# Two groups of on-chip buffers moved to other start addresses: activations by 96 bytes, shared buffers by 160 bytes in each partition

## The chip, the cores and the metric

The kernel runs on one core of one Trainium2 chip. Its time is device microseconds (us) of one launch, the median of three runs. The on-chip memory SBUF has 128 partitions; a buffer lies at the same byte address in each of them, and the kernel writes these addresses by hand.

## The reference

The program is a small language model's forward pass over 256 tokens of width 1024, in float32, three layers in a row.

- Layer 1: RMS norm; one projection to 2840 columns; compressed, selected and windowed attention (8 heads) beside differential attention (4 heads); output projection; squared-ReLU MLP of width 4096.
- Layer 2: the same frame with 16-head block attention and a second MLP of width 4096.
- Layer 3: one projection to 7696 columns that feeds a gated linear recurrence (1280 channels, a convolution of 4 taps, a scan) and 16-head forgetting attention; two branch projections, a merge and an output projection; then a gated feed-forward part of width 3072 with a convolution of 3 taps; a last norm.

```python
for i in range(DEPTH):                                   # layers 1 and 2
    hn = rms_norm(x, norm_mix[i])
    mix = even_mixer(hn, ...) if i % 2 == 0 else odd_mixer(hn, ...)
    x = x + mix
    x = x + sqrelu_mlp(rms_norm(x, norm_mlp[i]), mlp_w1[i], mlp_w2[i])
x = rms_norm(x, norm_final)
# layer 3
proj = rms_norm_2(x, mix_norm_pre) @ w_in
y_a = gelu(ga) * rg_lru(causal_dwconv(xa, ...), ...)
y_b = forgetting_attention(q, k, v, f_logit + b_forget)
merged = sigmoid(g_a + b0) * (y_a @ w_proj_a) + sigmoid(g_b + b1) * (y_b @ w_proj_b)
x = x + rms_norm_2(merged @ w_out, mix_norm_post)
up = causal_dwconv(rms_norm_2(x, ffn_norm_pre) @ w_up, ...)
x = x + rms_norm_2((gelu(gate) * val) @ w_down, ffn_norm_post)
```

Nearly all of the work is the product of activations with weight matrices.

## The kernel before

**Weights.** Every weight matrix is cut into slabs of 1024 rows by 256 columns (1 MiB). SP's queue loads each slab into one of five slots of `raw` (`slab`, L471), ScalarE writes a rounded copy to `w_hi` (`split_hi`, L698), and VectorE writes the remainder `w_lo = raw - w_hi` over the raw slab (`split_lo`, L1026). Both halves have the type float32r.

**Activations.** They are split in the same way into a high and a low part, float32r too, in one of a few buffers: `act_hi`/`act_lo` (the inputs of nearly all first products), `hid_hi`/`hid_lo` (the MLP's hidden layer), `mix_hi`/`mix_lo` (attention output), `ya_hi`/`ya_lo`, `m2_hi`/`m2_lo` (named `m_hi`/`m_lo` in the rows) and `h2_hi`/`h2_lo` (named `h_hi`/`h_lo`).

**The product.** TensorE runs `gemm` (L1532), one slab a call. For each of the slab's eight chunks of 128 rows and for both halves of its columns it issues three matmuls, high by high, high by low and low by high, each preceded by its own load of a 128x128 block into the array:

```python
passes = ((w_hi, x_hi), (w_hi, x_lo), (w_lo, x_hi))
...
ins = pe.matmul(dst, lhs, rhs, ...)      # L1561; lhs is loaded, rhs streams past it
```

Normally `lhs` is a block of the weights and `rhs` is a 128x256 piece of the activations (1024 bytes in each partition). Where `tok_major` is set, the roles are exchanged: `lhs` is a block of the activations and `rhs` is a 128x256 piece of the weights. This is so for the values of the attention stages, the gates, and the whole last stage (`f_dn`). In the rows a name such as `ps_gemm<-act_hi,w_hi` is the normal form and `ps_gemm<-w_hi,act_hi` the exchanged one (the streaming operand stands first). A full slab is 48 matmuls. All of these products have the line L1561 in the profile.

**Order.** The order of the work is written out by hand for each engine; semaphores join the engines. In the three attention stages a table (`FILL`) puts pieces of the products between the scores, transposes and value products of each pair of heads, so that TensorE works while VectorE and ScalarE do the softmax. Outside of them (the MLPs, the projections of layer 3, its feed-forward part) the products follow one another with no other work on TensorE.

**Placement.** `place` (L176 and what follows) puts each buffer at `top[0]`, the next free byte rounded up to 32. First come the weights' slots, the bias, `x`, small tables, then `act_hi` and `act_lo`. Behind them lie 8 KiB of scratch (`tmp0`: `sq`, `sq_sum`, `up_r`, `up_q`, `prob`, `sig_a`, `f_logsig`), and from `arena` on about 70 KiB that the stages share in turn (`hid`, `mix`, `ya`, `m2`, `h2`, queries, keys, values, `xa_pad` and all others made by `ar`). The starts that the code gives:

| buffers | start before | remainder by 64 | by 128 |
|---|---|---|---|
| `w_lo`, `w_hi` | 16512, 57472 | 0 | 0 |
| `eps_ones` (a table of constants) | 130272 | 32 | 96 |
| `act_hi`, `act_lo` | 132800, 140992 | 0 | 64 |
| `tmp0` and all in it | 149184 | 0 | 64 |
| `arena`; `hid_hi`, `mix_hi`, `h2_hi`, `xa_pad` start there | 157376 | 0 | 64 |

All pieces that a matmul of L1561 reads lie a multiple of 512 bytes behind its buffer's start, so that a buffer's remainders are those of all its pieces.

Of the kernel before, what the change touches and what calls it, by code (L numbers as in the profile page):

```python
# [141 lines left out]
def build(nc, ctx, t, out):  # L142
# [5 lines left out]
    top = [base]  # L148

    def place(name, shape, dt=F32, at=None):  # L150
        size = int(np.prod(shape[1:])) * 4
        if at is None:
            at = top[0]
            top[0] = -(-(at + size) // 32) * 32
        return nc.alloc_sbuf_tensor_at(name, shape, dt, offset=at)
# [23 lines left out]
    rs_o = place("ffn_rs", [P, TB])  # L179
    fcq = place("f_cum_q", [P, TB, 16])  # L180
    fw = place("conv_f", [P, 4, 2 * NH2])
    act_hi = place("act_hi", [P, NX, T], F32R)
    act_lo = place("act_lo", [P, NX, T], F32R)
    tmp0 = top[0]
    arena = tmp0 + 8 * K
    assert arena + 70 * K <= 229344, arena + 70 * K

# [1740 lines left out]
```

## Time and profile before

| | |
|---|---|
| median of three runs | 1252.53 us (1247.95 to 1256.39) |
| the profiled execution's own time | 1244.96 us |
| its span, first to last instruction | 1243.2 us |
| mean granted TensorE clock | 0.962 of full speed |
| TensorE matmul / weight load busy | 1158.9 us (93%) / 1116.4 us (90%) |
| VectorE, ScalarE, GpSimd busy | 796.4, 586.6, 147.4 us |
| read from HBM | 192.86 MB, 156 GB/s over the span |

A matmul counts as busy from its start to its modelled end (about 0.28 us), and the next one starts before that end. What a matmul costs in a long row of them is therefore the distance between two starts, which is had from the number of matmuls in a stretch, not from the busy time.

### The profile page before, as it was taken

How to read it: one execution, taken by the hardware profiler on the slowest of the kernel's cores; microseconds unless marked ns; L12 is line 12 of the kernel's file. 1: busy time of each engine (PE TensorE's matmuls, PEld its weight loads, DVE VectorE, ACT ScalarE, POOL GpSimd, SP SyncE). 2: the span in 40 equal slices, each digit the busy share in tenths (PEclk: the TensorE clock that was granted, in tenths of full speed). 3: DMA queues.
4: the chain of work that ended last, by engine and by line, in shares of the span. 5: the costliest groups of instructions: out<-in, count | busy, mean ns of one | idle time of the engine just before them, and what ended most of it. 6: DMA issues, size and time to landing. Idle time of an engine off the chain costs nothing.

```text
span 1243.2 us, 21636 instructions
## 1 busy us (share of the span) xinstructions
PE 1158.9 (93%) x9407; PEld 1116.4 (90%) x9407; DVE 796.4 (64%) x1131; ACT 586.6 (47%) x823; POOL 147.4 (12%) x83
## 2 busy tenths in 40 slices
PE   6799888999999999999999999999977979999997
PEld 5798668999999899999999999999975879999997
DVE  6436546877454665787654788776554677888852
ACT  4146654443334464444433556654344446666531
POOL 3000004000031000400022202400060021110100
PEclk8879889999999999999999999999988998999999
DMA  8934205555555443656555371654951353656550
GB/s 218 221 101 136 69 2 162 177 187 187 188 186 169 136 137 106 200 179 194 181 192 178 121 206 41 197 158 150 318 189 35 103 169 105 201 173 218 177 195 36
DMA packets 198771, 195.71 MB, mean 157 GB/s; under 512 B 9692, under 2 KB 196757, under 8 KB 198677
## 3 DMA queue, kind: packets, MB, share of 16 engines
q1 hardware_dynamic: 194116, 190.72, 49.2%
q10 hardware_dynamic: 4560, 3.62, 1.0%
q8 instruction: 74, 1.21, 0.4%
q14 instruction: 21, 0.16, 0.0%
HBM read 192.86 MB, written 1.46 MB: 156 GB/s over the span
## 4 chain that ended last, share of the span: by engine, by line
PE 77%; DVE 9%; SPq 5%; DMA 3%; POOL 2%; ACT 1%; issue 1%; DVEq 0%; ACTq 0%; POOLq 0%
PE ps_gemm L1561 67%; PE ps_score L1626 2%; PE ps_out L1653 2%; DVE w_lo L1026 2%; PE ps_trans L1638 2%; PE ps_score L1837 2%; DMA f_bias<-cum_scr 2%; DVE prob L1066 1%; SPq L509 1%; PE ps_gemm L1731 1%; POOL f_bias L657 1%; SPq L553 1%; DVE act_lo L1032 1%; DMA raw<-in_w_in 1%; DVE prob L1095 1%
## 5 line engine op out<-in xcount | busy, mean ns | idle before, releaser
L1561 PE MATMUL ps_gemm<-act_hi,w_hi 128*128 128x256 f32 x1640 | 467.3, 285 | 27.0 <-DVE act_lo L1032 21.2
L1561 PE MATMUL ps_gemm<-act_lo,w_hi 128*128 128x256 f32 x1640 | 461.8, 282 | 0.0
L1561 PE MATMUL ps_gemm<-act_hi,w_lo 128*128 128x256 f32 x1640 | 461.5, 281 | 0.0
L1026 DVE TENSOR_TENSOR w_lo<-raw,w_hi 128x2048 fp32r<-128x2048 f32 (+2 forms) x179 | 409.5, 2295 | 69.1 <-ACT w_hi L698 68.7
L698 ACT ACTIVATE w_hi<-raw 128x2048 fp32r<-128x2048 f32 (+2 forms) x179 | 332.7, 1862 | 204.0 <-DMA raw<-in_mlp_w 97.9
L1561 PEld LDWEIGHTS ps_gemm<-act_hi,w_hi 128*128 128x128 f32 x1640 | 311.6, 190 | 35.8 <-issue 30.4
L1561 PEld LDWEIGHTS ps_gemm<-act_lo,w_hi 128*128 128x128 f32 x1640 | 311.6, 190 | 0.3
L1561 PEld LDWEIGHTS ps_gemm<-act_hi,w_lo 128*128 128x128 f32 x1640 | 311.3, 190 | 0.2
L1561 PE MATMUL ps_gemm<-hid_hi,w_hi 128*128 128x256 f32 x512 | 143.1, 280 | 0.0
L1561 PE MATMUL ps_gemm<-hid_hi,w_lo 128*128 128x256 f32 x512 | 143.1, 279 | 0.0
L1561 PE MATMUL ps_gemm<-hid_lo,w_hi 128*128 128x256 f32 x512 | 142.8, 279 | 0.0
L1561 PEld LDWEIGHTS ps_gemm<-hid_hi,w_lo 128*128 128x128 f32 x512 | 96.2, 188 | 0.0
L1561 PEld LDWEIGHTS ps_gemm<-hid_lo,w_hi 128*128 128x128 f32 x512 | 96.0, 188 | 0.0
L1561 PEld LDWEIGHTS ps_gemm<-hid_hi,w_hi 128*128 128x128 f32 x512 | 95.9, 187 | 0.0
L755 ACT ACTIVATE prob<-prob,nmin 128x256 f32<-128x256 f32 (+3 forms) x128 | 54.3, 425 | 41.4 <-DVE nmin L1066 41.2
L623 POOL TENSOR_TENSOR sq_sum<-x 128x512 f32<-128x512 f32 x5 | 12.8, 2570 | 488.9 <-DVE x L1230 251.9
L831 ACT ACTIVATE hid_hi<-up_r 128x512 fp32r<-128x512 f32 x32 | 20.2, 632 | 93.3 <-DVE up_r L1248 93.3
L1066 DVE CUSTOM_DVE_ANT_0 prob<-ps_score,bias 128x128 f32<-128x128 f32 (+1 forms) x96 | 25.7, 323 | 48.6 <-PE ps_score L1626 48.6
L1561 PE MATMUL ps_gemm<-w_hi,act_hi 128*128 128x256 f32 (+1 forms) x192 | 55.9, 291 | 0.0
L1561 PE MATMUL ps_gemm<-w_hi,act_lo 128*128 128x256 f32 (+1 forms) x192 | 55.1, 287 | 0.0
L1561 PE MATMUL ps_gemm<-w_lo,act_hi 128*128 128x256 f32 (+1 forms) x192 | 55.0, 286 | 0.0
L1561 PE MATMUL ps_gemm<-w_hi,h_hi 128*128 128x256 f32 x192 | 53.1, 277 | 0.0
(282 smaller groups left out, 1738.1 us busy)
## 6 DMA issues: line engine op xcount, KB each, us to landing
raw<-in_mlp_w SPq DMA_DIRECT2D x64, 1024.0 KB, 5.4
raw<-in_w_in SPq DMA_DIRECT2D x30, 1024.0 KB, 5.7
raw<-in_w_up SPq DMA_DIRECT2D x24, 1024.0 KB, 5.2
raw<-in_od_w_in SPq DMA_DIRECT2D x12, 1024.0 KB, 5.1
raw<-in_w_down SPq DMA_DIRECT2D x12, 1024.0 KB, 5.2
raw<-in_ev_w_in SPq DMA_DIRECT2D x9, 1024.0 KB, 8.4
raw<-in_w_proj_a SPq DMA_DIRECT2D x8, 640.0 KB, 4.3
raw<-in_ev_w_out SPq DMA_DIRECT2D x4, 1024.0 KB, 5.3
```

The costliest lines, as they stand in the source:

```text
L509: sp.dma_start(cw1[:, i, :, :], t[f"ev_cmp_w1_{name}"][0].rearrange("(m p) j -> p m j", p=P)).then_inc(ld["cw"], 16)
L623: ins = pool.tensor_tensor(dst, v, v, ALU.mult)
L698: act.activation(w_hi[:, slot, 0:k, 0:n], raw[:, slot, 0:k, 0:n], ACT.Copy).then_inc(hi_done, 1)
L755: ins = act.activation(v, v, ACT.Exp, scale=-1.0, bias=nmin[:, k, b:b + 1], accum_out=psum_[:, k, b:b + 1])
L831: act.activation(hid_hi[:, 2 * j:2 * j + 2, :], up_r[:, j % 2, :, :], ACT.Square).then_inc(hid_h, 1)
L1026: dve.tensor_tensor(w_lo[:, slot, 0:k, 0:n], raw[:, slot, 0:k, 0:n], w_hi[:, slot, 0:k, 0:n].bitcast(F32), ALU.subtract).then_inc(w_ready, 1)
L1066: ins = dve.tensor_tensor_reduce(out=prob[:, k % PB, c0:c0 + w], in0=ps_s[:, m, c0:c0 + w], in1=u["bias"][b], scale=1.0, scalar=u["init"], ...
L1561: ins = pe.matmul(dst, lhs, rhs, start=(first and opens and i == 0 and half == 0 and q == 0), stop=(last and closes and i == len(ks) - 1 a ...
L1626: ins = pe.matmul(ps_s[:, m, c0:c0 + w], u["q"][:, b * P:(b + 1) * P], u["k"][b], start=True, stop=True)
L1638: ins = pe.transpose(ps_t[0:w, 0 if pr["kind"] == "diff" else m, q * P:(q + 1) * P], prob[:, k, c0:c0 + w], ident[:, :])
L1653: ins = pe.matmul(ps_o[r, pr["seq"] % 2, o0:o1], v, probs_t[0:k, m, c0:c1], start=(pr["start"] and q == 0), stop=(pr["stop"] and q == 1), ...
L1837: ins = pe.matmul(ps_s[:, j % 2, i * T:(i + 1) * T], gw[:, i, c, j - c + 1, :], xc[:, c, :], start=(q == 0), stop=(q == len(srcs) - 1))
```

## The change

Two lines. Ahead of `act_hi` the running address grows by 96 bytes, and ahead of the scratch by another 64, so that the scratch and the arena stand 160 bytes further on.

```diff
@@ -179,9 +179,10 @@
     rs_o = place("ffn_rs", [P, TB])
     fcq = place("f_cum_q", [P, TB, 16])
     fw = place("conv_f", [P, 4, 2 * NH2])
+    top[0] += 96
     act_hi = place("act_hi", [P, NX, T], F32R)
     act_lo = place("act_lo", [P, NX, T], F32R)
-    tmp0 = top[0]
+    tmp0 = top[0] + 64
     arena = tmp0 + 8 * K
     assert arena + 70 * K <= 229344, arena + 70 * K
```

After it `act_hi` starts at 132896 (remainder 32 by 64, 32 by 128), `tmp0` at 149344 and `arena` at 157536 (both remainder 32 by 64, 96 by 128). Weights, `x` and the tables stay. No instruction is added, removed or moved on any engine: each of the five streams has the same instructions in the same order, with other addresses.

## Rows read from the trace of the kernel before

**Rows 1.** The page's busy times, and its chain of waits by engine.

```profile
PE 1158.9 (93%) x9407; PEld 1116.4 (90%) x9407; DVE 796.4 (64%) x1131; ACT 586.6 (47%) x823; POOL 147.4 (12%) x83
...
PE 77%; DVE 9%; SPq 5%; DMA 3%; POOL 2%; ACT 1%; issue 1%; DVEq 0%; ACTq 0%; POOLq 0%
```

**Rows 2.** The chain in order of time: start us, length us, what (layer 2's MLP).

```profile
517.22 175.27 PE ps_gemm L1561 x1488
```

**Rows 3.** Groups of L1561's matmuls, whole span; count, busy us, mean ns, idle before.

```profile
L1561 PE MATMUL ps_gemm<-act_hi,w_hi 128*128 128x256 f32 x1640 | 467.3, 285 | 27.0 <-DVE act_lo L1032 21.2
L1561 PE MATMUL ps_gemm<-hid_hi,w_hi 128*128 128x256 f32 x512 | 143.1, 280 | 0.0
L1561 PE MATMUL ps_gemm<-w_hi,act_hi 128*128 128x256 f32 (+1 forms) x192 | 55.9, 291 | 0.0
L1561 PE MATMUL ps_gemm<-w_hi,h_hi 128*128 128x256 f32 x192 | 53.1, 277 | 0.0
...
L1561 PE MATMUL ps_gemm<-mix_hi,w_hi 128*128 128x256 f32 x128 | 38.0, 297 | 2.1 <-DVE x L1230 1.2 <-DVE mix_lo L1123 0.9
...
L1561 PE MATMUL ps_gemm<-ya_hi,w_hi 128*128 128x256 f32 x80 | 22.1, 276 | 0.0
...
L1561 PE MATMUL ps_gemm<-m_hi,w_hi 128*128 128x256 f32 x64 | 18.0, 281 | 0.6 <-DVE m_lo L1450 0.6
```

**Rows 4.** Busy time by stretch: start:end, length; us and count per engine; clock, DMA.

```profile
214.50:299.00 84.50, 84.50 (x720) 84.50 (x719) 67.85 (x62) 38.84 (x32) 0.00 (x0) 1.00 0.59 187
299.10:389.40 90.30, 90.30 (x770) 90.30 (x768) 42.63 (x22) 33.60 (x23) 15.31 (x5) 1.00 0.58 187
517.20:601.80 84.60, 84.60 (x721) 84.60 (x720) 67.85 (x62) 38.91 (x32) 0.00 (x0) 1.00 0.59 187
601.90:692.20 90.30, 90.30 (x769) 90.30 (x768) 42.62 (x22) 34.99 (x27) 15.32 (x5) 1.00 0.58 187
...
775.20:808.60 33.40, 33.40 (x286) 33.40 (x285) 25.98 (x20) 21.26 (x21) 14.03 (x4) 1.00 0.61 190
838.90:914.80 75.90, 75.90 (x671) 75.84 (x670) 48.51 (x38) 34.05 (x29) 10.84 (x3) 1.00 0.78 241
...
1038.00:1167.80 129.80, 129.80 (x1105) 129.80 (x1104) 111.73 (x150) 83.22 (x95) 14.24 (x11) 1.00 0.58 190
...
1186.30:1234.80 48.50, 48.50 (x430) 48.50 (x429) 16.96 (x11) 11.93 (x14) 0.00 (x0) 1.00 0.32 106
```

**Rows 5.** The same view, two slabs of layer 2's attention stage, normal form, `act`.

```profile
415.60:420.40 4.80, 4.80 (x45) 4.80 (x44) 0.00 (x0) 2.65 (x3) 0.00 (x0) 1.00 0.67 217
422.20:427.00 4.80, 4.80 (x43) 4.80 (x43) 4.22 (x11) 3.68 (x9) 0.00 (x0) 1.00 0.68 215
```

**Rows 6.** TensorE in order of time: start us, length us; from `f_up` to `f_dn`.

```profile
1167.16 0.28 PE L1561 MATMUL ps_gemm<-act_hi,w_hi 128*128 128x256 f32 x1
...
1167.87 0.29 PE L1561 MATMUL ps_gemm<-w_hi,h_hi 128*128 128x256 f32 x1
...
1168.11 0.28 PE L1561 MATMUL ps_gemm<-w_lo,h_hi 128*128 128x256 f32 x1
...
1168.68 0.28 PE L1561 MATMUL ps_gemm<-w_hi,h_lo 128*128 128x256 f32 x1
```

**Rows 7.** L1561 in the gates' slab (24 streamed columns): us and count, PE and PEld.

```profile
42.60:46.40 3.80, 3.80 (x37) 3.80 (x36) 1.00 1.06 290
```

**Rows 8.** Line L1597, a plain float32 product with constants: min/median/max ns.

```profile
L1597 PE MATMUL ps_score<-sq,ones x4: 379/379/379, 700.7 to 701.4; 128*128 128x256 f32 x4
...
L1597 PE MATMUL ps_score<-sq_sum,eps_ones x4: 379/379/379, 701.6 to 702.3; 128*128 128x256 f32 x4
```

**Rows 9.** ScalarE and VectorE reading `xa_pad`, whose rows are 1036 bytes apart: min/median/max ns.

```profile
L872 ACT ACTIVATE xc<-xa_pad,par x10: 584/588/602, 711.2 to 732.8; 128x256 f32<-128x256 f32 x10
...
L1336 DVE SCALAR_TENSOR_TENSOR xc<-xa_pad,par,xc x30: 475/479/484, 713.3 to 736.7; 128x256 f32<-128x256 f32 x30
```

## The prediction

> **What bounds the kernel now.** I read the page's busy times and its chain of waits first [rows 1]: TensorE is busy for 93% of the span and holds 77% of the chain; no other engine holds a tenth. The chain in order of time shows how long the unbroken pieces are: the whole second MLP is one piece of 175.27 us and 1488 matmuls of L1561 [rows 2]. In such a piece nothing is waited for, and its length is the number of matmuls times the distance between two starts. So next I read how many there are [rows 3]: each row stands for three equal groups (high by high, high by low, low by high), so L1561 has 3 x (1640 + 512 + 192 + 192 + 128 + 80 + 64) = 8424 matmuls. Then I read the distance, from the stretches that hold nothing else [rows 4]. A matmul is 0.28 us long and is counted wherever it overlaps a stretch, so 2.4 more are counted than start in it. In 1038.00 to 1167.80 us 1102.6 start, 0.1177 us apart. In 1186.30 to 1234.80 us 427.6 start, **0.1134 us** apart, and in 838.90 to 914.80 us 668.6, 0.1135 us apart. The clock is granted in full (2.4 GHz) in all of them. So the same instruction has two paces, 0.1177 and 0.1134 us, 4.3 ns apart, and this is the one thing in the trace that an address could plausibly touch for a great many instructions.
>
> The pace isn't a matter of what is waited for, nor of the form alone. Two slabs 7 us apart, both with `act` streaming past the weights, both with DMA at about two thirds, start 45 - 2.4 = 42.6 and 43 - 2.4 = 40.6 matmuls in the same 4.80 us [rows 5]: 0.1127 and 0.1182 us, one at each pace within the error of one count. A pace, once there, holds for hundreds of matmuls: the first MLP's 720 and 770 matmuls and the second's 721 and 769 are all slow, the last stage's 430 all fast [rows 4]. And it can turn where the operands change their roles: at the end of `f_up`, with `act` streaming, six starts take 0.71 us (0.118 each), and a few matmuls after `h` and the weights have exchanged roles, five take 0.57 us (0.114 each) [rows 6]. In the buffers' starts only the roles differ there: the streaming operand's remainder by 128 goes from 64 to 0, the loaded one's from 0 to 64. I read this as two reads of the same memory, the weight load's and the streaming one's, which run side by side and settle into one of two steady rhythms. Which of them they settle into depends on where they meet, and so on both addresses and on how the stretch began.
>
> **The change, part by part.** No instruction is added, removed or moved, and no semaphore or queue changes. What is left is four prices of an address.
>
> *ScalarE, VectorE, GpSimd and DMA on moved buffers: nothing.* `xa_pad` has rows of 1036 bytes, so its ten reads by ScalarE begin at many remainders, and last 584 to 602 ns; VectorE's 30 reads, shifted by 4 bytes a tap, last 475 to 484 ns [rows 9]. A start that is a multiple of 32 bytes can't cost more than these, under 4%. VectorE's busy time is 111.73 of 129.80 us in its densest long stretch [rows 4], so even 4% on it stays under TensorE.
>
> *Plain float32 products: nothing.* `eps_ones` already starts at remainder 32 by 64 as the loaded operand, and its product takes 379 ns, as the one with `ones` (remainder 0) does [rows 8]. It is the only matmul operand at such a start, and no row shows a streaming operand or a float32r one there.
>
> *The slow stretches.* The six slow stretches of [rows 4] count 720 + 770 + 721 + 769 + 286 + 1105 = 4371, less 6 x 2.4, so 4357 starts in 512.9 us. At the fast pace they would take 4357 x 4.3 ns = 18.7 us less. Nothing else would hold them back: at 0.1134 us a slab of 48 takes 5.44 us, and VectorE needs 111.73 / 23 = 4.86 us a slab in `f_up`, the most of any. The other 8424 - 4357 - 1096 = 2971 matmuls (1096 start in the two fast stretches) lie among the attention stages and the heads of the others. 2971 x 4.3 ns = 12.8 us is their most; some are fast already, and others cover a softmax that would then be waited for, so I take a third, 4.3 us. **Upper value of a gain: 18.7 + 12.8 = 31.5 us; taken, where the pace turns: 23.0 us.** There is a floor below which this can't go: with only 24 columns to stream, the weight loads alone set the distance, 3.80 us for 37 - 2.3 = 34.7 starts, about 0.110 us [rows 7]. So the fast pace is all but the floor, and there is no third, still faster one of weight.
>
> *The fast stretches.* If they turn slow, 1096 x 4.3 ns = 4.7 us are lost, and with the fast ones among the 2971 at most about 8 us.
>
> The position is lopsided: four fifths of what I can see is slow, and 23 us stand against 8. Both remainders change by the same half step (32 by 64) against the unmoved weights, in all products. The role change of [rows 6] shows that the pair of addresses has a say, so I hold a turn for more likely than not; but the trace doesn't show any product at the new distance, so the direction is judged by where there is room.
>
> A rule of the Trainium skill speaks against all of this. Its page "TensorE: Matmul & The Clock Gate" (the part on loading the weights) says that the array has two independent SBUF read ports and that loading the next weights takes nothing from the running matmul. By it the two reads never meet, and the change is worth nothing. The trace doesn't settle it, since the same pair of reads goes at 0.1127 and 0.1182 us a matmul at unchanged addresses [rows 5]: something between them isn't free, whatever it is.
>
> **The sum.** It is made against the profiled execution, 1244.96 us (span 1243.2 and 1.8 around it): -23.0 gives 1222 us. That execution lies 7.6 us under the median of the three runs, 1252.53. I carry the difference over to the median: 1252.5 - 23.0 = 1229.5, so **1230 us**, 1.8% less.
>
> **The rivals.**
>
> 1. *The pace turns fast nearly everywhere* (the forecast). 1252.5 - 18.7 to - 31.5, so 1221 to 1234. For it: room, and a pace that holds for hundreds of matmuls once entered. Against it: fast stretches exist at the old addresses too, so addresses aren't the whole cause. Chance 0.38.
> 2. *It turns for one of the two groups only.* With `act` alone: 720 + 721 + 286 + 1105 less 4 x 2.4 = 2822 matmuls, 12.1 us, so about 1239. With the arena's alone: 770 + 769 less 4.8 = 1534, 6.6 us, so 1246. For it: after the change the groups differ by 128 (32 against 96). Chance 0.12, half of it (where `act` turns) with 1% or a little over.
> 3. *Nothing.* The paces are set by how each stretch starts, as [rows 5] allow, and their mix stays: 1252.5, within the 1248 to 1256 that the runs show. The rule of the two read ports ends here as well. Chance 0.30.
> 4. *The fast stretches turn slow.* 1252.5 + 4.7 to 8, so 1257 to 1260. Chance 0.05.
> 5. *Slower.* A 1024-byte streaming read that begins at remainder 32 by 64 touches one block of 64 bytes more than before, and the two reads fall into a third, slower rhythm. Its place is every matmul of L1561. Priced at one more step of the size seen, 8424 x 4.3 ns = 36 us: 1289. It decides from 3 us over the fast-slow balance on: at 1.5 ns a matmul (12.6 us) it is the 1% that can be seen. For it: nothing in [rows 8], which has a loaded float32 operand; against it only that row. Chance 0.15.
>
> **How the numbers follow.** Faster by over 1% (which is about the least that runs of this kernel, 1247.95 to 1256.39, can tell from no change): 0.38 of case 1 and 0.06 of case 2, 0.44. Within 1%: 0.06 + 0.30 + 0.05, so 0.41. Slower: 0.15. The likeliest single case is the first, and 1230 is its time; its own range is 1221 to 1234. The range that should hold the time in 8 of 10 must take in cases 1 to 4 and leave out 5: 1221 to 1261 us.
>
> **What would show each step.** In the profile of the changed kernel the windows of the first and second MLP and of `f_up` are counted again. At the fast pace 84.60 us hold 84.60 / 0.1134 + 2.4 = 748 matmuls in place of 721, and 129.80 us hold 1147 in place of 1105; the chain's piece for the second MLP is 1488 x 4.3 ns = 6.4 us shorter, 169 us. Were the count unchanged in `act` windows and higher in `hid` windows, or the reverse, it is case 2. A count under 717 in 84.60 us is case 5. The last stage should keep 430 in 48.50 us. The rows of ScalarE and VectorE [rows 9] and the 379 ns of L1597 should stay. The prediction is wrong in its base if the pace turns and the time doesn't: then something that I hold for covered (the weight splits on VectorE, the loads) ends the stretches.

## The result, and the profile after

The changed kernel takes **1257.22 us** (median of 19 runs, 1254.26 to 1266.69), the kernel before 1250.18 us (19 runs beside them, 1247.11 to 1257.88). The ratio is 1.0063, 95% interval 1.0045 to 1.0081: slower by 0.6%. The forecast was 1230 us, 1.8% faster. The direction was wrong, and the time lies inside the stated range only because that range held the small losses too. Ratios here are of runs not over 1.5% above the fastest of their kernel; for one kernel below (both groups by 128 bytes), whose runs scatter by more than that, it leaves real ones out, and its medians stand beside it.

The page of the changed kernel, busy times and the chain by engine (compare [rows 1]), and the chain's piece for the second MLP (compare [rows 2]):

```profile
PE 1166.6 (93%) x9407; PEld 1123.9 (89%) x9407; DVE 796.4 (63%) x1131; ACT 586.9 (47%) x823; POOL 147.3 (12%) x83
...
PE 79%; DVE 10%; DMA 4%; ACT 2%; POOL 2%; issue 1%; SPq 1%; ACTq 0%; DVEq 0%; POOLq 0%
...
523.64 175.38 PE ps_gemm L1562 x1488
```

VectorE, ScalarE and GpSimd are busy as before to within 0.3 us; TensorE is busy for 7.7 us more. The second MLP's 1488 matmuls take 175.38 us, as before (175.27).

The same view as [rows 4] (start:end, length; busy us and count of PE, PEld, DVE, ACT, POOL; clock; DMA share; GB/s), the same stages in the changed kernel: first `hid` stage, second `act` stage, a stage of layer 3 that was fast before, `f_up`, `f_dn`:

```profile
304.00:394.30 90.30, 90.30 (x765) 90.30 (x764) 42.39 (x22) 33.63 (x23) 15.31 (x5) 1.00 0.57 187
523.80:608.40 84.60, 84.60 (x723) 84.60 (x722) 68.09 (x63) 38.80 (x32) 0.00 (x0) 1.00 0.59 187
...
891.00:923.00 32.00, 32.00 (x275) 32.00 (x275) 19.87 (x12) 13.99 (x8) 10.28 (x3) 1.00 0.98 303
1046.50:1176.30 129.80, 129.80 (x1084) 129.80 (x1083) 109.76 (x146) 82.39 (x94) 14.19 (x11) 1.00 0.57 187
1197.50:1246.00 48.50, 48.50 (x418) 48.50 (x418) 16.90 (x11) 11.86 (x14) 0.00 (x0) 1.00 0.32 105
```

With 2.4 taken from each count, the distance between two starts is 118.4 ns (117.7 before), 117.4 (117.7), 117.4 (113.5), 120.0 (117.7) and 116.7 ns (113.4). Neither old pace is in any of these stretches. Over all products at the full clock (taken from the start of each to the start of the next, where one of this line follows another at once), the mean of 8168 distances is 118.25 ns; before it was 116.84 over 8121. That is 1.41 ns x 8121 = 11.5 us on TensorE, of which `act` in the normal form has 4735 x 0.98 ns = 4.6 us, `act` exchanged 511 x 4.7 ns = 2.4, `h` 573 x 3.3 ns = 1.9, `ya` 239 x 5.0 ns = 1.2, `hid` 1534 x 0.55 ns = 0.8, and `mix` and `m` 0.5 together. The profiled executions are 12.6 us apart (1244.96 and 1257.54), the medians 7.0. The profiled one of before was faster than all 19 beside the changed kernel: its first MLP begins at 206.7 us, that of the changed kernel at 211.4, and those of two kernels below (all by 96 bytes, both groups by 256), whose long stretches have the paces of before, at 211.6 and 210.2. In the long stretches without a break (both MLPs, the exchanged `act` and the `ya` products of layer 3, `f_up`, `f_dn`) the changed kernel's profile is 6.7 us longer, nearly the 7.0 of the medians.

### The profile page after: what moved, and what is told of

Read it like the earlier page. It is cut to its first block, busy times and chain, and to the rows that moved or that the text cites. A ratio compares the mean times of both kernels' runs of the same rounds, so it can differ in the third digit from the quotient of the medians.

```text
span 1255.7 us, 21636 instructions
## 1 busy us (share of the span) xinstructions
PE 1166.6 (93%) x9407; PEld 1123.9 (89%) x9407; DVE 796.4 (63%) x1131; ACT 586.9 (47%) x823; POOL 147.3 (12%) x83
## 4 chain that ended last, share of the span: by engine, by line
PE 79%; DVE 10%; DMA 4%; ACT 2%; POOL 2%; issue 1%; SPq 1%; ACTq 0%; DVEq 0%; POOLq 0%
PE ps_gemm L1562 69%; DVE w_lo L1027 3%; PE ps_score L1627 2%; PE ps_out L1654 2%; PE ps_trans L1639 2%; DMA f_bias<-cum_scr 2%; PE ps_score L1838 1%; DVE act_lo L1033 1%; DVE prob L1067 1%; PE ps_gemm L1732 1%; POOL f_bias L658 1%; SPq L554 1%; DMA raw<-in_w_in 1%; DVE prob L1096 1%; DMA raw<-in_ev_w_in 1%
```

## The experiments

The word **distance** below means the start of the streamed piece minus the start of the loaded block, modulo 256. The weights start at 128 modulo 256 and `act` and the arena started at 192. So the distance was 64 in the normal form and 192 in the exchanged one. After the change it is 160 and 96 for `act`, 224 and 32 for the arena.

For all kernels but the maps and the one by 128 bytes I show the same three stretches: first `hid` stage (normal form), `f_up` (`act`, normal), `f_dn` (`h`, exchanged). In 85.00 us a pace of 117.8 ns gives a count of 724, 113.3 ns one of 752; in 120.00 us 1021 and 1061 (120.0 ns: 1002); in 45.00 us 384 and 399. The kernel before, in this view:

```profile
301.00:386.00 85.00, 85.00 (x724) 85.00 (x724) 40.96 (x20) 30.85 (x18) 15.31 (x5) 1.00 0.57 186
1040.00:1160.00 120.00, 120.00 (x1022) 120.00 (x1021) 103.97 (x141) 77.17 (x89) 12.94 (x10) 1.00 0.58 188
1188.00:1233.00 45.00, 45.00 (x399) 45.00 (x398) 15.26 (x11) 11.18 (x13) 0.00 (x0) 1.00 0.30 100
```

### A map of paces without the model

```diff
-    (all stages of the model)
+    for wc, xc, tok, mode in SERIES:     # weights' start, activations' start, form, lead-in
+        ...                              # then 48 matmuls, three passes, as one slab
```

> This kernel leaves out all of the model: it only runs series of 48 float32r matmuls (three passes, a slab as in the kernel, the same 128x128 loads and 128x256 streams) between buffers at chosen starts, each series three times with another lead-in (a wait of about a microsecond; four plain float32 matmuls of 128 rows; six of 64 rows). Weights at remainder 0, 32 or 64 by 128, activations at eight starts 32 bytes apart, both forms. Theory A (the two addresses set a menu of paces): at starts that are multiples of 64 the distance between matmuls is 113.3 or 117.8 ns, at remainder 32 by 64 it is 116.7 to 120.0 ns and never 113.3, and the same pair of addresses gives the same one or two values under all three lead-ins. Theory B (start conditions alone): the paces are spread over the pairs without order, 113.3 ns appears at remainder 32 too, and the three lead-ins of one pair differ as much as two pairs do. Theory C (the reads never meet): one pace for all pairs, at or under 113.3 ns, since no other engine runs here.

The rows are TensorE in order of time (start, length, what). Each pair is the 7th and the last matmul of a series of 48, thus 41 distances. First distance 0 (activations at 640 modulo 1024), then distance 64 (at 704), third lead-in both:

```profile
50.73 0.28 PE L79 MATMUL ps_gemm<-xhi_a,whi_a 128*128 128x256 f32 x1
...
55.65 0.28 PE L79 MATMUL ps_gemm<-xhi_a,wlo_a 128*128 128x256 f32 x1
...
95.85 0.28 PE L79 MATMUL ps_gemm<-xhi_c,whi_a 128*128 128x256 f32 x1
...
100.50 0.28 PE L79 MATMUL ps_gemm<-xhi_c,wlo_a 128*128 128x256 f32 x1
```

4.92 / 41 = 120.0 ns, and 4.65 / 41 = 113.4 ns. Worked out in this way for every series (ns for the three lead-ins, rounded; the one series that began at half clock is left out):

```
distance       0            32           64           96           128          160          192          224
normal     -    120 120  117 118 117  118 118 113  120 120 120  120 119 119  117 117 119  113 118 113  118 118 118
exchanged  120  120 120  117 118 117  118 118 118  120 120 120  119 119 119  117 120 119  113 118 113  118 118 118
```

The two lines draw on the same values in each column, though in one the weights are loaded and in the other streamed. With the weights moved too (to 160 and 192), four more pairs, each in both forms, at distances 0, 32, 64, 192 and 224, gave the values of their columns again. So theory A stands: the distance sets a menu of one to three paces. The lead-in has a part in the pick, since one pair of addresses gives two values, but it isn't all of it: at distance 192 the three lead-ins gave 113, 118, 113 ns with one pair of addresses and 118, 118, 113 with another. Theory C falls: nothing else runs on the core here, and the same pair of instructions still takes 113.3 to 120.0 ns by its addresses. One part of what I expected under A was wrong: that 113.3 ns never occurs at remainder 32 by 64. It does where both operands have it (weights at 160, activations at 736, distance 192).

Two distances have the same menu and not the same odds. Over this map and the finer one below, distance 64 gave 113.3 ns in 1 series of 15, distance 192 in 9 of 15. That fits the kernel before, whose normal form (64) is nearly all slow and whose exchanged form (192) is mostly fast.

### Everything moved by 96 bytes, the weights too

```diff
-    base = 16512
+    base = 16512 + 96
```

> Every buffer, the weights too, moves by 96 bytes: the distances between all pairs of buffers are those of before, but all starts are at remainder 32 by 64. If the distance between the two operands decides: paces 113.3 and 117.8 ns and the time of before within 2 us. If each operand's own remainder by 64 decides (a read that begins inside a block of 64 bytes): no 113.3 ns in any product, paces of 117 to 120 ns or more, as both operands are now off, and 7 to 20 us longer.

```profile
306.00:391.00 85.00, 85.00 (x724) 85.00 (x724) 40.84 (x20) 30.70 (x18) 15.31 (x5) 1.00 0.58 186
1046.00:1166.00 120.00, 120.00 (x1022) 120.00 (x1020) 103.93 (x139) 77.16 (x89) 12.94 (x10) 1.00 0.59 188
1194.00:1239.00 45.00, 45.00 (x399) 45.00 (x399) 15.74 (x11) 11.18 (x13) 0.00 (x0) 1.00 0.32 104
```

1252.76 us against 1253.40; ratio 0.9994 (0.9974 to 1.0015). The counts are those of before. Every float32r operand now starts at remainder 32 by 64, and at these distances it costs nothing. The prediction's fifth rival (a read that begins inside a block of 64 bytes) is refuted, and it is the distance, not the address, that counts.

### Both groups by 256 and by 192 bytes

```diff
+    top[0] += 256        # in the other kernel: += 192
     act_hi = place("act_hi", [P, NX, T], F32R)
```

> Both groups move by 256 bytes. Theory A: every distance modulo 256 is as before, so the same menu, hid and f_up at 117.8, h and ya at 113.3 ns, and the time of before within 3 us. Rival (the absolute address or a longer period counts): other picks, such as hid at 113.3 ns or values off 113.3 and 117.8.

```profile
304.00:389.00 85.00, 85.00 (x724) 85.00 (x723) 41.58 (x21) 30.81 (x18) 15.32 (x5) 1.00 0.57 186
1046.00:1166.00 120.00, 120.00 (x1022) 120.00 (x1021) 103.96 (x141) 77.22 (x88) 12.97 (x10) 1.00 0.58 189
1193.00:1238.00 45.00, 45.00 (x400) 45.00 (x399) 15.56 (x11) 11.18 (x13) 0.00 (x0) 1.00 0.30 102
```

1252.60 us against 1252.54; ratio 1.0001 (0.9978 to 1.0025), and the counts of before. A whole period of 256 changes nothing. The picks repeat too: the profiles of before, of all by 96 and of both by 256 have ten stretches of over 100 matmuls in a row, and show the same pace in nine of them (the tenth, 131 matmuls of layer 3, went at 117.8, 117.8 and 113.3 ns). So at these distances they are hardly drawn anew by chance in each execution.

> Both groups move by 192 bytes: distance 0 modulo 256 in both forms, all starts multiples of 64. Theory A: 120.0 ns in all products, none at 113.3 or 117.8; by 8121 matmuls x 3.2 ns about 20 to 26 us over before, the slowest placement. Rival (a start that is a multiple of 64 is what gives the good menu): 113.3 and 117.8 ns as before and no change.

```profile
309.00:394.00 85.00, 85.00 (x710) 85.00 (x710) 40.09 (x19) 29.25 (x17) 15.33 (x5) 1.00 0.55 181
1060.00:1180.00 120.00, 120.00 (x1002) 120.00 (x1002) 101.55 (x138) 75.57 (x88) 12.95 (x10) 1.00 0.57 182
1210.00:1255.00 45.00, 45.00 (x377) 45.00 (x376) 15.64 (x11) 11.15 (x13) 0.00 (x0) 1.00 0.31 103
```

Distance 0 in both forms: 120.1, 120.0 and 120.1 ns. 1270.13 us against 1252.54; ratio 1.0147 (1.0114 to 1.0180), 17.6 to 18.4 us slower. All starts are multiples of 64, so that isn't what makes a placement good. The expectation was 20 to 26 us, from a sum of 25 us on TensorE. By the profiles 15.9 us are in the long stretches without a break; of the other 9, in the attention stages and the heads, little comes out in the time.

### The two groups apart

```diff
     # the arena alone               # act alone
-    tmp0 = top[0]                   +    top[0] += 96      (ahead of act_hi)
+    tmp0 = top[0] + 160             -    tmp0 = top[0]
+                                    +    tmp0 = top[0] + 160
```

> act_hi and act_lo stay, the scratch and the arena move by 160 bytes as in the change. Theory A: hid 118.3, ya 118.3, h 116.7 ns as in the changed kernel, act products at 113.3 or 117.8 ns as before; by the counts (1534 x 0.55, 239 x 5.0, 573 x 3.3 ns and the small ones) about 4 us longer than before. Theory B: no change within 2 us.

```profile
304.00:389.00 85.00, 85.00 (x721) 85.00 (x720) 40.43 (x19) 30.38 (x19) 15.32 (x5) 1.00 0.57 185
1046.00:1166.00 120.00, 120.00 (x1021) 120.00 (x1021) 103.95 (x141) 77.15 (x89) 12.94 (x10) 1.00 0.58 188
1194.00:1239.00 45.00, 45.00 (x388) 45.00 (x387) 15.65 (x11) 11.15 (x13) 0.00 (x0) 1.00 0.31 103
```

`hid` at 118.3 and `h` at 116.7 ns as in the changed kernel, `act` as before. Ratio 1.0032 (1.0010 to 1.0054): 4.0 us, as expected. The medians are closer, 1254.08 against 1253.40, since seven of its 12 runs lie at 1251 to 1255 us and five at 1258 to 1261. In the profile the long stretches are 5.0 us longer than before.

> act_hi and act_lo move by 96 bytes as in the change, the scratch and the arena by 256, which leaves their distance modulo 256 at 64. Theory A: act products at 117.3 to 120.0 ns (exchanged 119.5), every other product at 113.3 or 117.8 ns. By the counts act costs 4735 x 1.0 + 511 x 4.8 ns = 7 us; if hid and h also pick what they had before, the ratio is 1.003 to 1.006, and with the arena's own 1.0032 it makes up the 1.0063 of the change. If hid or h pick the other of their two values, the time is up to 7 us less or 3 us more. Rival (each group's share is not separable, something shared such as a bank of the arena and act together): act at 113.3 or 117.8 ns.

```profile
305.00:390.00 85.00, 85.00 (x724) 85.00 (x724) 41.42 (x21) 30.80 (x18) 15.30 (x5) 1.00 0.56 186
1048.00:1168.00 120.00, 120.00 (x1014) 120.00 (x1013) 102.97 (x139) 76.31 (x89) 12.89 (x10) 1.00 0.57 185
1196.00:1241.00 45.00, 45.00 (x400) 45.00 (x399) 16.11 (x11) 11.18 (x13) 0.00 (x0) 1.00 0.32 106
```

`act` leaves its old paces (here 118.6 ns), `hid` and `h` keep theirs. Ratio 1.0017 (0.9999 to 1.0035), under the 1.003 to 1.006 that I expected, and by itself not clear of no change; in the profile the long stretches are 3.0 us longer than before. In `f_up` it picked 118.6 where the changed kernel picked 120.0 ns: 1103 x 1.4 ns = 1.5 us. The two parts come to 1.0049, within the interval of the whole (1.0045 to 1.0081).

An earlier form of this experiment moved the arena by 128 in place of 256:

> act_hi and act_lo move by 96 bytes as in the change, the scratch and the arena by 128, so that these keep their remainder by 128. Theory A: the act products take their new paces (117.3 to 120.0 ns; 4735 normal ones cost 1.0 ns each, 511 exchanged ones 4.7 ns), the hid, ya and h products stay at 117.8, 113.3 and 113.3 ns; about 7 us longer than before. Theory B: the mix of 113.3 and 117.8 ns stays in all of them, no change within 2 us.

```profile
303.00:388.00 85.00, 84.89 (x750) 84.69 (x748) 40.30 (x21) 32.27 (x22) 15.32 (x5) 1.00 0.61 196
1036.00:1156.00 120.00, 120.00 (x1014) 120.00 (x1013) 102.97 (x138) 76.31 (x88) 12.88 (x10) 1.00 0.57 185
1185.00:1230.00 45.00, 45.00 (x384) 45.00 (x383) 14.88 (x10) 11.15 (x13) 0.00 (x0) 1.00 0.29 97
```

I had taken 128 for a whole period, and it isn't one: the arena's distance went from 64 to 192 in the normal form and from 192 to 64 in the exchanged one. `hid` picked 113.5 ns, and the ratio is 0.9970 (0.9955 to 0.9986). `h` (distance 64) went at two paces, the first three slabs of `f_dn` at 113.4 ns and the rest at 117.8:

```profile
1168.00:1181.00 13.00, 13.00 (x117) 13.00 (x116) 8.47 (x7) 6.18 (x4) 1.29 (x1) 1.00 0.59 192
```

Between the two TensorE does other work for 1.8 us (transposes of `x`, 1180.82 to 1182.49). So what comes between can change the pick at unchanged addresses, as it did in [rows 5]: the fast slab there follows an exchanged one at 113.3 ns without a break, the slow one comes behind a score product. The ratio was a miss of the expectation, and the first sign that the good pace can be had in the MLPs.

### Both groups by 128 bytes

```diff
+    top[0] += 128
     act_hi = place("act_hi", [P, NX, T], F32R)
```

> Both groups move by 128 bytes, so streaming start minus loaded start (call it the distance, modulo 256) goes from 64 to 192 in the normal form and from 192 to 64 in the exchanged one. Theory A (the distance modulo 256 sets the menu of paces): the menu stays 113.3 and 117.8 ns for all products; hid at 113.3 ns as in the kernel with act at 96 and the arena at 128; which of the two act takes is open, so 6 us (hid alone) to 28 us (all) under before. Rival (remainder modulo 128 is all that counts): the same picks as before, same time within 2 us.

The first and the second `act` stage of the MLPs, then the first and the second `hid` stage:

```profile
225.80:301.80 76.00, 76.00 (x648) 76.00 (x647) 60.99 (x58) 35.57 (x29) 0.00 (x0) 1.00 0.60 189
527.90:603.90 76.00, 76.00 (x673) 76.00 (x672) 62.66 (x59) 35.75 (x29) 0.00 (x0) 1.00 0.61 194
304.80:395.10 90.30, 90.03 (x765) 89.82 (x763) 42.37 (x23) 33.59 (x23) 15.31 (x5) 1.00 0.56 187
604.00:694.30 90.30, 88.89 (x782) 88.51 (x782) 45.90 (x29) 38.62 (x34) 18.19 (x8) 1.00 0.60 196
```

The same stage with the same addresses goes at 117.7 ns in layer 1 and at 113.3 ns in layer 2. Both paces are on this distance's menu, and each long stretch picks one. I had expected 113.3 ns for all of `hid`; the first MLP missed it. `h` and `ya`, now at distance 64, went at 117.8 ns. The 12 runs scatter from 1229.13 to 1254.32 us (standard deviation 7.1 us), the 23 of the kernel before beside them from 1244.64 to 1260.09 (3.7 us). The ratio is 0.9919 (0.9881 to 0.9957), that of the medians 1247.04 / 1252.54 = 0.9956. It is a somewhat faster placement on the mean, and an unsteady one. As the fastest run shows, my forecast's 1230 us can occur at distances 64 and 192. That it needs the fast pick in most stretches is my reading; that run has no profile.

### A finer map, and a version made from it

The starts between multiples of 32 (the buffers themselves stay at multiples of 32; the operand is a view that begins some elements into its buffer):

> Leaves out all of the model, as the first map; weights at 128 modulo 1024, activations at starts that are 16 bytes off a multiple of 32 (656, 688, 720, 752, 784, 848), at 708 (4 bytes behind the start of before) and at 960 (256 behind it), both forms, three lead-ins each. Theory A: 960 gives 113.3 and 117.8 ns like 704; the others lie between 113.3 and 120 ns. If the reads are by blocks of 64 or 32 bytes, 708 costs one more block and leaves the menu of 704; if the phase in time is what counts, 708 stays near it. A pace under 113.3 ns anywhere would point to a better placement.

At distance 112 in the normal form (activations at 752) the 7th and the last matmul of the third series:

```profile
113.10 0.28 PE L80 MATMUL ps_gemm<-xhi_d,whi_a 128*128 128x256 f32 x1
...
117.76 0.28 PE L80 MATMUL ps_gemm<-xhi_d,wlo_a 128*128 128x256 f32 x1
```

4.66 / 41 = 113.7 ns; the other two lead-ins gave 113.7 and 113.3. It is the only start in all maps that is near 113.3 ns under all three. In the normal form distances 16, 48, 80, 144 and 208 gave 116.6 to 120.0 ns; 708 (4 bytes behind the start of before) gave 117.8 three times, 960 gave 117.8 three times in the normal form and 113.3, 117.8, 113.3 in the exchanged one. The symmetry of the two forms doesn't hold here: exchanged, distance 112 gave 116.7, 120.0 and 120.0, and distance 208 gave 117.7, 123.2 and 123.5 ns (normal 116.6, 119.1, 119.1), which is above the 120 that I had expected as the most.

> Leaves out all of the model, as the maps before; activations at 744, 748, 756 and 760 modulo 1024 (4 and 8 bytes about 752, weights at 128), and at 728, 712, 776 and 816. Theory A with a smooth dependence on where the two reads meet: the neighbours of 752 are at 113.3 ns too, or within a few ns of it. If the blocks read are 16 bytes long: 756 and 760 behave as 752, 744 and 748 as 736 (120.0 ns).

The point is narrow. In the normal form 744 gave 120.0 ns, 748 120.0, 756 121.6 to 121.9, 760 119.9 to 121.1; 712, 728, 776 and 816 gave 118.9 to 121.2. In the exchanged form only 728 (distance 168) came near, with 113.8, 116.6 and 113.6. Neither of my two readings (a smooth dependence, blocks of 16 bytes) fits 756 and 760.

```diff
+    top[0] += 32; shift[0] = 16           # every buffer from act_hi on: a view 16 bytes into it
     act_hi = place("act_hi", [P, NX, T], F32R)
...
-    h2_hi = ar("h2_hi", [P, NH2, T], 0, F32R)
+    h2_hi = h2("h2_hi", [P, NH2, T], 0, F32R)     # at arena + 224, no view: distance 192 as before
...                                                # h2_lo likewise; the buffers behind it 256 bytes further on
```

> A version built from the map: the activations' buffers stand 48 bytes further on than before (start 16 bytes off a multiple of 32, distance 112 modulo 256 in the normal form), while h, which is used only in the exchanged form, keeps its remainder (distance 192). Theory A: all normal products at 113.3 ns whatever the lead-in (before: 117.3 on average), h at 113.3 ns, the exchanged act products at about 120 ns (before 114.6); 6980 x 3.9 ns less 511 x 5.4 ns on TensorE, of which 15 to 25 us come out at the end: 1228 to 1238 us, 1.2 to 2% under before. Rival (the map's value holds only while the other engines are silent): 117 to 118 ns in the model's stretches and no gain.

```profile
300.00:383.00 83.00, 83.00 (x735) 83.00 (x734) 39.89 (x19) 31.78 (x22) 15.32 (x5) 1.00 0.60 197
1034.00:1150.00 116.00, 116.00 (x1026) 116.00 (x1025) 103.54 (x139) 76.02 (x88) 14.32 (x11) 1.00 0.62 201
1172.00:1217.00 45.00, 45.00 (x385) 45.00 (x384) 15.52 (x11) 11.15 (x13) 0.00 (x0) 1.00 0.30 102
```

At 117.8 ns the first two stretches would hold 707 and 987. `hid` and `act` in the normal form are at 113.3 ns, in every long stretch of the profile. `h` turned to 117.8 ns though its distance is as before. **1234.19 us against 1249.15, ratio 0.9872 (0.9841 to 0.9903)**: this beats the kernel before by 1.3% and the changed one, measured beside other runs, by about 1.8%. The expected 113.3 ns held in all long stretches of the normal form; `h` missed it, which costs 573 x 4.4 ns = 2.5 us. By the positions of the stages in the two profiles the two MLPs and `f_up` are 18.3 us shorter than before and `f_dn` is 2.5 us longer. The rest, the attention stages above all, is some 2 us longer in spite of the faster products. There the chain goes through the softmax on VectorE and the loads too; I did not follow it further.

## Why the prediction was wrong

*What bounds the kernel, and that the pace is what an address can touch:* right. The time from one start to the next was what changed; 11.5 us on TensorE, of which 7 show in the medians.

*That the pace depends on both addresses:* right, and more exactly so than I had it. At starts that are multiples of 32 it is the difference of the starts modulo 256 (all at once by 96, nothing; both by 256, nothing; both by 192, 1.5% slower). *"The role change of [rows 6] shows that the pair of addresses has a say"* was right for another reason than I gave: I compared remainders by 128, by which the roles of 0 and 64 are alike. By 256 they are 64 and 192. That the cause is two reads of one memory getting in each other's way fits all runs, but none shows it.

*The slow stretches, "At the fast pace they would take 4357 x 4.3 ns = 18.7 us less":* **this is the step that failed.** The pace did turn, but not to the fast one. I took the two paces of before for all there are and asked only which of the two the new addresses would pick. But the two are the menu of distances 64 and 192. The new distances 160, 96, 224 and 32 have menus of their own, 116.7 to 120.0 ns, and 113.3 isn't on any. The slow `act` stretches went to 117.4 and 118.7 ns (no gain to speak of) or to 120.0 (`f_up`), `hid` to 118.3. In place of -23.0 us the two groups gave +4.0 and +2.1, and both together +7.0.

*"There is no third, still faster one of weight" and "four fifths of what I can see is slow":* the floor was right, since 113.3 is the least that any map showed (the gates' slab of [rows 7] has 111.7 ns from start to start, 43.05 to 46.40 us for 30 of them; my count made it 110), but room below says nothing on where a new distance falls. Of the eight distances that are multiples of 32 only two have 113.3 on their menu, and before had exactly these two. From there a blind move by an odd multiple of 32 bytes had little to gain (117.4 or 116.7 in place of 117.8) and all of the fast stretches to lose.

*The fast stretches, 4.7 to 8 us lost:* they did lose, by `h` 1.9, `ya` 1.2, the exchanged `act` 2.4 and the 287 `act` matmuls ahead of the third attention stage 1.1 us, together 6.6. Rival 4 said 4.7 to 8 us more, and 7.0 were measured, but by a mechanism a little beside it: not to 117.8 ns but to each distance's own value. That 1257.22 also lies in its 1257 to 1260 is in part luck, as the kernel before came out at 1250.18 and not at the 1252.5 that the rival starts from.

*ScalarE, VectorE, DMA and plain float32 products: nothing.* Right: VectorE is busy for 796.4 us before and after, the reads of `xa_pad` last 584 to 604 and 476 to 485 ns, and the product of [rows 8] 379 ns.

*The rule of the two read ports.* In the maps nothing but TensorE runs, and the distance alone moves the pace from 113.3 to 120.0 ns. The Trainium skill's page "TensorE: Matmul & The Clock Gate" (the part on loading the weights) says that loading the next weights takes no read bandwidth from the running matmul; read as the prediction read it, that the placement makes no difference, it does not hold for these float32r matmuls, and the measurement decides.

What stays open is what picks within a menu. The lead-in has a part (one pair of addresses at 113.3 and 117.8 ns in one map), and it seems that the pace of the stretch ahead has one too: at distance 192, `h` was fast in the four profiles where `f_up` went at 117.8 or 118.6 ns, and slow in the last one, where `f_up` went at 113.3. Each placement has one profile, and three of those four have the same distances, so this is an observation and not a proof. Nor is it shown why distance 112, 16 bytes off a multiple of 32, is steady at 113.3 ns and its neighbours aren't.

## What to carry to other kernels

Where TensorE is the bound, count the matmuls in a stretch and divide, rather than read their busy time; two values for one instruction at one clock are a sign of a rhythm that a placement may change. Before moving a buffer by a few bytes, map the paces with nothing but the two operands: eight starts with three lead-ins take under 200 us on the chip and would have told the sign here. Ask of a new placement which values it can take at all, not only which of the known ones it will pick, and test it in the kernel, since the map doesn't say what a long stretch will pick.

## What the runs showed of the hardware that I had not expected

- A float32r matmul of 128x256 with its own weight load takes 113.3 to 120.0 ns from start to start at 2.4 GHz (granted clock 1.00), by the difference of the two start addresses modulo 256, where both are multiples of 32: 120.0 at 0 and at 96, 118.6 to 120.0 at 128, 117.3 to 120.0 at 160, 118.3 at 224, 116.7 or 117.8 at 32, 113.3 or 117.8 at 64 (113.3 in 1 series of 15) and at 192 (9 of 15). Other starts gave up to 123.5 ns.
- A move of all buffers, the weights too, by 96 bytes (starts at remainder 32 by 64) changes neither pace nor time (0.9994).
- A pace holds through a long uninterrupted stretch, 1103 matmuls in `f_up`; behind 1.8 us of transposes it can be another (113.4, then 117.8 ns in `f_dn` at distance 64); and one placement can give the same stage 117.7 ns in one layer and 113.3 ns in the next. Whole runs of one such placement scattered from 1229 to 1254 us.
